# Two transformer blocks in one launch: where the first output products of the second block's mixer stand among its attention groups

## What is computed

```python
def _diff_attention(q, k, v, lam, subln_g, lambda_init):      # 4 heads, two score maps each
    p = _masked_softmax(s1, mask) - lam * _masked_softmax(s2, mask)
    o = einsum('bhqk,bkhe->bqhe', p, v)
    o = _rmsnorm(o, subln_g, SUBLN_EPS) * (1.0 - lambda_init)

def _mla(cq, ckv, kr, cos, sin, ...):                          # 4 latent heads
    sc = (einsum('bqhd,bkhd->bhqk', qnb, kn) + einsum('bqhr,bkr->bhqk', qrb, kr)) * scale
    o = einsum('bhqk,bkhe->bqhe', _masked_softmax(sc, mask), v)

def _hybrid_mixer(h, ...):
    y_a = _diff_attention(...)          # 256 columns
    y_b = _mla(...)                     # 256 columns
    y_c = _mamba2(...)                  # 512 columns, ends in a norm
    return concatenate([y_a, y_b, y_c], axis=-1) @ w_out

x = x + g_m * _rmsnorm(y, norm_g[l, 1])
```

## Time and profile before

| | us |
|---|---|
| three executions | 3128.38, 3133.84, 3138.25 |
| median | 3133.84 |
| the profiled execution, its own time | 3130.37 |
| its span in the trace | 3128.60 |
| PE busy in the span | 2908.3 |
| DVE, POOL, ACT busy | 1787.2, 931.1, 756.2 |
| mean granted clock of PE, share of full speed | 0.951 |

### The profile page before, as it was taken

How to read it: one execution, slowest core, us unless ns; L and a number is a source line. 1 busy time by engine, 2 the same in 40 slices (tenths; PEclk the granted TensorE clock), 3 DMA queues, 4 the chain that set the end, 5 groups by cost and what they waited for, 6 DMA issues and landing times.

```text
span 3128.6 us, 33693 instructions
## 1 busy us (share of the span) xinstructions
PE 2908.3 (93%) x12126; PEld 2133.1 (68%) x12126; DVE 1787.2 (57%) x3803; ACT 756.2 (24%) x1781; POOL 931.1 (30%) x794
## 2 busy tenths in 40 slices
PE   8888999999997899999989988999999998899997
PEld 4354688888544578888854456888884454688886
DVE  2673469388367447938854545877824634551433
ACT  2354310000235431000022353201112335320111
POOL 0301224443330124444412202344440400344442
PEclk9989999999998799999989988999999998899998
DMA  6115034244221013434421101254421210122221
GB/s 256 64 61 215 28 138 166 101 148 170 91 80 61 1 55 121 175 108 156 154 76 56 61 27 68 108 183 186 156 100 57 59 50 23 40 94 96 81 81 54
DMA packets 45412, 313.28 MB, mean 100 GB/s; under 512 B 5424, under 2 KB 5552, under 8 KB 31040
## 3 DMA queue, kind: packets, MB, share of 16 engines
q1 hardware_dynamic: 42912, 306.88, 27.0%
q10 hardware_dynamic: 2304, 4.20, 0.6%
q0 software_dynamic: 32, 0.07, 0.0%
HBM read 298.53 MB, written 2.10 MB: 96 GB/s over the span
## 4 chain that ended last, share of the span: by engine, by line
PE 70%; DVE 18%; ACT 6%; issue 3%; DMA 1%; POOL 1%; DVEq 0%; SPq 0%; ACTq 0%; POOLq 0%
PE bank L1114 39%; PE bank L1094 9%; PE bank L1440 7%; PE bank L1168 3%; DVE nw L2067 3%; PE bank L1264 2%; DVE sel L2304 2%; DVE m L2303 1%; PE bank L1307 1%; DVE SPT L2368 1%; ACT SPT L1756 1%; PE bank L1294 1%; PE bank L1229 1%; PE bank L1567 1%; DMA sel<-in_mod_pieces 1%
## 5 line engine op out<-in xcount | busy, mean ns | idle before, releaser
L1000 POOL TENSOR_TENSOR SPT<-ring 128x512 f32<-128x512 f32 (+2 forms) x140 | 175.2, 1252 | 956.3 <-DMA ring<-in_slabs 493.0
L1114 PE MATMUL bank<-U,ring 128*128 128x256 f32 x1728 | 412.2, 384 | 10.8 <-DVE U L2101 10.5
L1114 PEld LDWEIGHTS bank<-U,ring 128*128 128x128 f32 x1728 | 332.8, 193 | 58.4 <-DVE U L2101 12.5
L2067 DVE SCALAR_TENSOR_TENSOR nw<-sel,c,nw 128x256 f32<-128x256 f32 x504 | 321.7, 638 | 31.2 <-DMA sel<-in_mod_pieces 13.5
L1114 PE MATMUL bank<-U,SPT 128*128 128x256 f32 x1296 | 312.5, 381 | 3.0 <-POOL SPT L1005 3.0
L1114 PEld LDWEIGHTS bank<-U,SPT 128*128 128x128 f32 x1296 | 247.4, 191 | 37.7 <-POOL SPT L1005 4.4
L1114 PE MATMUL bank<-hT,SPT 128*128 128x256 f32 x1088 | 257.1, 379 | 0.0
L1440 PE MATMUL bank<-hT,ring 128*128 128x512 f32 x544 | 249.7, 607 | 7.1 <-ACT hT L1873 7.1
L2127 DVE TENSOR_TENSOR rb<-bank,nw 128x256 f32<-128x256 f32 x108 | 45.5, 422 | 355.9 <-PE bank L1114 259.1
L1114 PE MATMUL bank<-hT,ring 128*128 128x256 f32 x1088 | 246.1, 379 | 0.0
L1114 PEld LDWEIGHTS bank<-hT,ring 128*128 128x128 f32 x1088 | 207.0, 190 | 28.0 <-DMA ring<-in_slabs 0.3
(11 more groups left out here) (344 smaller groups left out, 4501.9 us busy)
## 6 DMA issues: line engine op xcount, KB each, us to landing
ring<-in_slabs SPq DMA_DIRECT2D x86, 2048.0 KB, 8.0
sel<-in_mod_pieces SPq DMA_DIRECT2D x144, 512.0 KB, 4.5
ring<-in_slabs SPq DMA_DIRECT2D x8, 1536.0 KB, 7.0
ring<-in_slabs SPq DMA_DIRECT2D x8, 1280.0 KB, 8.3
tab<-U SPq DMA_DIRECT2D x40, 128.0 KB, 2.0
U<-in_slabs SPq DMA_DIRECT2D x2, 2048.0 KB, 22.5
tmp<-nw ACTq DMA_DIRECT2D x16, 256.0 KB, 2.9
ring<-in_slabs SPq DMA_DIRECT2D x2, 1808.0 KB, 11.7
```

Of the source, the lines that this page charges most:

```text
L1000: pool.tensor_tensor(e1, a21, a22, ALU.add).then_inc(*pool_order.up())
L1114: mm = pe.matmul(into[j][:, c:c + HALF], lhs[:, k, :], rhs[:, k, :], start=(begin and k == 0), stop=(end and k == kp - 1))
L2067: ins = dve.scalar_tensor_tensor(a, w[:, k, :], c[:, j:j + 1], a, ALU.mult, ALU.add)
```

## The change

The two woven stretches become one. The key tiles now take the positions from -0.02 to 0.33, the state-space norm -0.06 to 0.24, the eight `wo, 0` steps 0.33 to 1.01 and all slots 0.04 to 1.04.

```diff
     slots = group_slots2(range(len(GROUPS2)))
     keys = [c for n in range(14, 18) for c in tile2(n)]
-    o += woven((0.01, 1, keys), (-0.15, 0.53, [[("sz",)], [("sn", 0)], [("sn", 1)]]),
-               (0.1, 1, [c for slot in slots[:NM2] for c in slot]))
-    o += woven((0.25, 1, [[("wo", 0, n)] for n in range(KT)]), (-0.15, 1.07, [c for slot in slots[NM2:] for c in slot]))
+    o += woven((-0.02, 0.33, keys), (-0.06, 0.24, [[("sz",)], [("sn", 0)], [("sn", 1)]]),
+               (0.33, 1.01, [[("wo", 0, n)] for n in range(KT)]), (0.04, 1.04, [c for slot in slots for c in slot]))
     for n in range(KT):
```

## The result

The kernel after took 3144.27 us (median of 9, 3137.06 to 3151.53), the kernel before beside it 3133.84. One execution of the kernel before took 6482.63 us, far from all others, and is left out of the ratio, which is 1.0038, with an interval of 1.0021 to 1.0054. So the change costs 6.6 to 17 us. The forecast of 3136.2 and its range to 3142 were wrong; of the cases weighed, the rival with the clock falling at several tiles comes nearest.

A forecast was written before the change was run, and what follows sets the result against it. The prediction took a loop over DVE and ACT, not PE, to bound most of the group slots it read. Two layers of 0.2 + 1.0 = 2.4 us on the median 3133.84 gave 3136.2 us, range 3129 to 3142.

The forecast's parts named there:

- the rival with the clock falling at several tiles: Tiles 1, 2 and 3 run at 1.2 GHz on the path: 6.2 us per layer, 3147 to 3148; chance 0.12.
- Step 1: First key tiles and state-space norm: PE's wait for the squares falls from 1.66 to 0.4 us; -1.2 us per layer.
- Step 2: Tile 0 ahead of the scores of group 7: DVE takes those scores up later; +2.6 us per layer.
- Step 3: Tile 1 ahead of the scores of group 9: ACT's copy stands ahead of the norm of group 6; +0.4 us.
- Steps 4, 5 and 6: Tile 2 behind scores of group 10 +0.5 us; places given up behind scores of group 11 -1.5, transposes of group 13 -0.6.
- sum at full clock: The terms of all moved places per layer, before the clock term is added: +0.2 us.
- Step 7: Place given up behind the transposes of group 16: `tp` of group 17 waits for `cb` regardless; 0 us.
- they cost what they cost: Five of the eight product tiles go to places that held a tile before, so their cost stays unchanged.
- The clock term: One clock fall per layer, expected between tile 1 and tile 3, slowing part of tile 2 or 3; 1.0 us.
- The words come true: Tiles fill PE's waits and the end hangs on PE: about 8.5 us less per layer, 3117 in all; chance 0.05.

The follow-up runs named there:

- tile_7: The kernel before with one tile moved from behind the scores of group 11 to ahead of the scores of group 7; 3129.22 us.
- tile_10: The kernel before with the new key order and one tile moved from behind the scores of group 11 to behind those of group 10; 3130.24 us.
- fill_before: The kernel before with three product tiles that nobody reads added behind the scores of groups 8, 9 and 10; 3141.90 us.
- give_13: The kernel before with the tile behind the transposes of group 13 moved behind the scores of group 10; 3134.45 us.
- fill_late: The kernel after with three unread product tiles per layer at the places given up, groups 11, 13 and 16; median 3132.33 us, ratio 1.0006.
- the second profile: The kernel after, unchanged, run and profiled once more; median 3137.97 us, ratio 1.0019 to the kernel before.
- keys_tile_10: The same program as tile_10 run again: new key order, one tile moved, against the kernel before; median 3130.61 us, ratio 0.9990.
- keys_only: The kernel before with only the key tiles and state-space norm in the new order, product tiles at their old places; 3124.68 us.

## Why the prediction was wrong, by its steps

- **Step 1, keys, -1.2: right.** PE's wait for the squares fell from 1.66 to 0.44 us (forecast 0.4), and the stretch became 1.0 us shorter in this pair and 1.1 to 1.2 over all profiles. The row, as against the earlier trace rows:

```profile
1776.94 1.95 PE L1453 MATMUL bank<-sqb,cst 128*128 128x512 f32 x4 [0.44 <-ACT sqb L1834]
```

- **Step 2, tile 0 ahead of the scores of group 7, +2.6: right**, +2.69 in both layers and again in `tile_7` alone.
- **Step 3, +0.4: too much.** Slot 5 to 6 grew by 0.06 us, from 6.77 to 6.84. Without the tile it took 6.62 where the clock fell later (`tile_10`, `tile_7`), so the tile costs 0.2 us at most.
- **Steps 4, 5 and 6, +0.5, -1.5, -0.6: right**, with +0.49, -1.60 and -0.73. But step 5 stands under "sum at full clock" and is mostly a clock term: with tile 0 in its old place and at full clock the slot takes 5.92 us (`fill_before`) or 5.91 (`give_13`), so 1.1 of the 1.6 us are the half clock at tile 0 and 0.5 the tile and its copy.
- **Step 7 and "they cost what they cost": wrong.** That tiles 3 to 7, at places that held a tile before, keep their price held for the order and not for the clock.
- **The clock term, 1.0 per layer: the step that failed.** It measured 3.95 and 3.7 us. I looked for one fall between tile 1 and tile 3, where it did come, at tile 3 with 5.87 us. I did not ask what became of the 51 us at full clock behind it. The change takes away two tiles inside them, and tile 0, at whose end they began. I listed these three places only as gains, of 1.5, 0.6 and 0. What the runs showed: the clock falls there, and with the places filled by products that nobody reads the four slots are back at before's values (`fill_late`). The rule on pieces with waits between them, from the Trainium skill ("TensorE: Matmul & The Clock Gate", "HAM oscillation — how this bites in real kernels"), was quoted as making every thinned place a candidate. This trace agrees at the late places, where three of four falls begin behind a tile that was taken away, and I gave it the weight of one.
- **The rival with several slow tiles** had the sign, and nearly the size, but named tiles 1, 2 and 3; slow were 3, 5, 6 and 7, of which only 3, 5 and 7 cost time, and in the second profile tile 2 as well. Its 0.12 was too little, since the one trace at hand showed that a fall lasts 24 us where work is thin.
- **The sum.** With the measured clock term the same steps give -1.1 + 2.7 + 0.1 + 0.5 - 1.6 - 0.7 + 3.8 = 3.7 us per layer, 7.4 in all, so 3141. The two comparisons give 11.9 us (1.0038) and 6.0 (1.0019), the traces 7.7 and 6.3. What the first comparison has beyond 8 us is within its interval; no trace shows it in the stretch. So 3141 would have lain in the stated range and 3144.27 does not: the clock term used up the range, and some 3 us that no trace shows took the median over its end. Two numbers of the prediction don't follow from its own terms: 6.2 us per layer give 3146 and not 3147, and tile 0 at 1.5 us without a clock term gives -0.9 per layer and not -2.5, so a lower end of 3132 and not 3129.

"The words come true" fell with the first trace: PE's waits for `tp` and `pv` grew, from 8.7 to 10.9 us, although the early ones were filled. The waits of PE from the last key product to the last `ot` (us in all, times, longest), before, then after:

```profile
PE bank L1526 <- DVE SPT L2585: 4.9, 7, 1.3
PE bank L1540 <- ACT yB L1942: 3.8, 4, 1.8
```

```profile
PE bank L1525 <- DVE SPT L2584: 5.5, 9, 1.5
PE bank L1539 <- ACT yB L1941: 5.4, 4, 2.2
```

## What to carry to other kernels

An engine that waits is not one that has time to give: ask first whether it is in the loop that sets the slot, since half clock and waits outside it can be free (as in the slots 6 to 8 here), and a block put ahead of the loop's next step costs its full length less the slack there. When blocks move, price the places they leave as closely as those they enter, with the clock at both; a dense block may be what keeps the next one at full speed. Compare stretches between points that the change leaves alone, in more than one execution, when the effect is smaller than the scatter ahead of it.

## What the runs showed of the hardware

- Work that nobody reads shortened a stretch: 11 us more on PE per layer, and 88.4 became 86.5 and 87.1 us (`fill_late`). In another place the same filler lengthened it, from 83.5 to 86.9 (`fill_before`).
- The clock's fall is not fixed by the order of the work. The same program met it at different tiles in two executions and lost 1 to 2 us per layer by it (`tile_10`, `keys_tile_10`). With the old key order, and no tile up to there, it came 9.6 us behind the last keys (`before`, `fill_before`) or 5 (`give_13`); with the new one 9.5 us in the first layer of `keys_only` and 14.2 in the second.
- The first fall goes together with the length of the key stretch ahead of it, which goes with the half clock in it (0.97 and 0.94 in the two windows of `keys_only` above). In all 13 stretches in which no tile stands ahead of the fall: old order, 54.8 to 54.9 us and a fall at 9.6 us (4), 53.5 to 53.6 and 5.1 to 5.4 (2); new order, 53.6 to 53.7 and 14.2 to 14.3 (5), 52.4 and 9.5 to 9.7 (2). So it is not scatter alone. Why they go together stays open: I have no run in which the clock ahead of the stretch was varied alone. The later falls differ between two executions even where the first is at the same place (`tile_10`, `keys_tile_10`), so a count of falls per layer can be given for an order of work only as a likelihood.
- One program reached the start of the stretch at 1751.7 us in one execution and at 1760.7 in another. These 9 us are more than the change is worth.
